# A near mask on GpSimd, a second bank for small tiles' transposes, and outputs weighted on ScalarE in the sparse attention

## What is computed

```python
logits = jnp.einsum('bqgrd,bqkgd->bqgrk', q_b, k_sel).astype(jnp.float32) * scale
bias = t5_table[t5_bucket(sel - tpos[None, :, None])]
logits = logits + bias.astype(jnp.float32)
logits = jnp.where(valid[:, :, None, None, :], logits, -jnp.inf)
p = jax.nn.softmax(logits, axis=-1).astype(v.dtype)
o = jnp.einsum('bqgrk,bqkgd->bqgrd', p, v_sel)
```

## Time and profile before

| | us |
|---|---|
| median of 3 executions (2685.77 to 2688.29) | 2685.83 |
| the profiled execution: its own time | 2684.7 |
| its span from first to last instruction | 2682.9 |
| of it `dsa_phase` | about 321 |
| PE busy in the span | 2594.0 (97%) |
| DVE, ACT, POOL busy | 1578.9, 1265.8, 1454.0 |

### The profile page before, as it was taken

One profiled execution on the slowest core, in us unless ns is written; L12 is line 12 of the kernel. 1 busy time (PEld: TensorE's weight loads), 2 busy tenths in 40 slices (PEclk: granted clock), 3 DMA queues, 4 the chain that ended last, 5 costly groups with the idle time before them and its releaser, 6 DMA issues. The chain is left out here.

```text
span 2682.9 us, 40475 instructions
## 1 busy us (share of the span) xinstructions
PE 2594.0 (97%) x14062; PEld 2256.1 (84%) x14062; DVE 1578.9 (59%) x2722; ACT 1265.8 (47%) x2823; POOL 1454.0 (54%) x1057
## 2 busy tenths in 40 slices
PE   6799899999999999999999999999999999999999
PEld 6699788898878888888789999999878788888877
DVE  5899877763665656556641114666448655556656
ACT  5678566662333333333445556777425333333332
POOL 2044433202557777777844444556217767777773
PEclk9999999999999999999999999999999999999999
DMA  5100000011111121111131110333311111111102
GB/s 182 47 25 24 29 9 5 28 60 48 48 48 48 55 69 48 47 47 47 40 129 48 48 48 21 80 91 80 114 48 48 48 47 47 63 47 51 60 29 94
DMA packets 77358, 147.24 MB, mean 55 GB/s; under 512 B 8528, under 2 KB 45568, under 8 KB 75552
## 3 DMA queue, kind: packets, MB, share of 16 engines
q1 hardware_dynamic: 77216, 145.38, 16.9%
HBM read 122.22 MB, written 13.69 MB: 51 GB/s over the span
## 5 line engine op out<-in xcount | busy, mean ns | idle before, releaser
L1116 DVE TENSOR_TENSOR XT<-XT,banks 128x1024 f32<-128x1024 f32 x176 | 214.6, 1220 | 210.4 <-PE banks L1021 210.3
L849 POOL TENSOR_TENSOR WL<-WF,WH 128x512 fp32r<-128x512 f32 x164 | 247.7, 1522 | 14.1 <-ACT WH L675 14.1
L849 POOL TENSOR_TENSOR WL<-WRB,WH 128x512 fp32r<-128x512 f32 x108 | 172.8, 1616 | 146.2 <-ACT WH L669 140.1
L987 PE MATMUL banks<-XH,WH 128*128 128x512 f32 x608 | 237.7, 391 | 5.0 <-ACT U L699 5.0
L849 POOL TENSOR_TENSOR WL<-WR,WH 128x512 fp32r<-128x512 f32 x98 | 198.8, 2051 | 76.6 <-ACT WH L669 76.6
L987 PE MATMUL banks<-XL,WH 128*128 128x512 f32 x608 | 237.2, 390 | 0.0
L987 PE MATMUL banks<-XH,WL 128*128 128x512 f32 x608 | 237.1, 390 | 0.0
L1021 PE MATMUL banks<-AH,WH 128*128 128x512 f32 x640 | 200.0, 394 | 6.1 <-DVE XT L1116 4.4
L1100 DVE SCALAR_TENSOR_TENSOR YG<-U,CONVW,YG 128x1023 f32<-128x1023 f32 x88 | 179.4, 2039 | 31.4 <-ACT YG L714 31.4
L1021 PE MATMUL banks<-AL,WH 128*128 128x512 f32 x640 | 197.5, 390 | 0.0
L1021 PE MATMUL banks<-AH,WL 128*128 128x512 f32 x640 | 197.1, 389 | 0.0
(11 more groups left out here) (442 smaller groups left out, 7525.1 us busy)
## 6 DMA issues: line engine op xcount, KB each, us to landing
WR<-in_up SPq DMA_DIRECT2D x44, 512.0 KB, 4.7
WRB<-in_up SPq DMA_DIRECT2D x44, 512.0 KB, 4.2
WF<-in_down SPq DMA_DIRECT2D x88, 256.0 KB, 2.6
HT<-HC SPq DMA_DIRECT2D x224, 64.0 KB, 2.0
QWR<-in_qkv SPq DMA_DIRECT2D x8, 1536.0 KB, 6.3
XT<-in_xT SPq DMA_DIRECT2D x16, 512.0 KB, 7.9
QWR1F<-in_qkv SPq DMA_DIRECT2D x4, 1536.0 KB, 6.4
spill<-XT SPq DMA_DIRECT2D x8, 512.0 KB, 11.0
```

Source lines behind the costliest of these rows:

```text
L849: pool.tensor_tensor(out_, src, hi.bitcast(F32), ALU.subtract).then_inc(signal, 1)
L987: mm = pe.matmul(BANK[bank], w[:, n, b * P:(b + 1) * P], x[:, b, :], start=(first and b == 0 and w is WH and x is XH[i]), stop=(b == 3 and ...
L1116: dve.tensor_tensor(c.XT[:, db, :], c.XT[:, db, :], DN[db % 2][:], ALU.add).then_inc(dn_free, 1)
```

## The change

Three moves, all in `dsa_phase`:

1. The mask of the near 256 keys is no longer added on PE. GpSimd adds it to the bias instead (`near_mask`, 96 instructions of 128 x 256, into a ring `NEAR` of 3), and `row_max` takes `NEAR` in place of `BB`. It waits for `near_ready`.
2. For tiles 0 to 2 the odd rounds (output and keys) are transposed into `TP[1]`, which those tiles leave unused, so that they need not wait for the copies of the queries out of `TQ`.
3. `output` on DVE keeps the reciprocal alone. ACT weighs the output (`weigh`), one instruction of 64 columns per head, ahead of `exp(g + 2)` in even steps.

```diff
+        NEAR = m.take("NEAR0", [P, AHEAD, W], F32)
...
-        RCP = m.take("RCP0", [P, 2], F32)
+        RCP = m.take("RCP0", [P, 2, 2], F32)
...
+        LAST_SIDE = 2
+        def on_side(g):
+            return g % 2 == 1 and place(g)[3] <= LAST_SIDE
+        def seat(g):
+            return TP[1] if on_side(g) else TQ
+        def seat_free(g):
+            earlier = [v for v in range(g) if has_round(v) and on_side(v) == on_side(g)]
+            return rounds_before(earlier[-1] + 1) if earlier else 0
...
+            def weigh(o):
+                act.wait_ge(rcp_done, o + 1)
+                act.wait_ge(pv_ready, 2 * o + 2)
+                for h in range(2):
+                    mm = act.activation(MO[:, o % 2, h * HD:(h + 1) * HD], OP[:, h * HD:(h + 1) * HD], ACT.Copy,
+                                        scale=RCP[:, o % 2, h:h + 1])
+                mm.then_inc(mo_ready, 1)
...
+                if h == 0 and g >= 2:
+                    weigh(g // 2 - 1)
                 if g + 2 < ALL:
                     exp(g + 2)
...
+            def near_mask(g):
+                p, k, s, i, h = place(g)
+                if i < FIRST_TOP:
+                    return
+                n, v = masked_before(g), (i + 1) * P - W
+                if p == 0:
+                    pool.wait_ge(mask_ready, i - FIRST_TOP + 1)
+                else:
+                    pool.wait_ge(b_masked, p)
+                if n >= AHEAD:
+                    pool.wait_ge(max_done, unmasked[n - AHEAD] + 1)
+                pool.tensor_tensor(NEAR[:, n % AHEAD, :], BB[p % 2][:, h, S - W:S],
+                                   MASK[:, SC_OFF[i] + v:SC_OFF[i] + v + W], ALU.add).then_inc(near_ready, 1)
...
             for t in range(EARLY, TT):
+                near_until(2 * t - 4)
                 scaled(t)
...
             for k in range(1, GROUPS):
+                base = 2 * UNITS * (k - 1)
                 for i in range(TT + 1):
+                    near_until(13 + 2 * (i // 2) if k == 1 else base + 2 * i + 3)
                     if i < TT:
                         raw_square(k * TT + i)
+                    if k > 1:
+                        near_until(base + 2 * i + 5)
                     if i >= 1:
                         root(k * TT + i - 1)
                     if i in (1, 2):
                         scaled(k * TT + i - 1)
                 for i in range(2, TT):
+                    near_until(base + UNITS + 2 * i + 2)
                     scaled(k * TT + i)
+            near_until(ALL)
...
-                hidden = i >= FIRST_TOP
-                if hidden:
-                    pe.wait_ge(mask_ready, i - FIRST_TOP + 1)
...
-                    mm = pe.matmul(blocks, q, keys[:, :, 1, :], start=False, stop=not covered)
-                    if covered:
-                        mm = pe.matmul(LG[g % 2][:, m0:b], c.IDB[:], MASK[:, SC_OFF[i] + m0:SC_OFF[i] + b],
-                                       start=False, stop=True)
+                    mm = pe.matmul(blocks, q, keys[:, :, 1, :], start=False, stop=True)
...
+                if i == 4 and g % 2 == 0:
+                    pe.wait_ge(turned_lo, rounds_before(g - 2 * (4 - LAST_SIDE) + 2))
...
+                    near_bias = NEAR[:, masked_before(g) % AHEAD, :]
+                    dve.wait_ge(near_ready, masked_before(g + 1))
...
                 dve.wait_ge(exp_done, 2 * o + 2)
-                dve.reciprocal(RCP[:], SUM[:, c0:c0 + 2]).then_inc(rcp_done, 1)
-                dve.wait_ge(rcp_done, o + 1)
-                dve.wait_ge(pv_ready, 2 * o + 2)
-                dve.tensor_tensor(MO[:, o % 2, :].rearrange("p (h d) -> p h d", h=2),
-                                  OP[:, 0:PAIR].rearrange("p (h d) -> p h d", h=2),
-                                  RCP[:].unsqueeze(2).to_broadcast([P, 2, HD]), ALU.mult).then_inc(mo_ready, 1)
+                if o >= 2:
+                    dve.wait_ge(mo_ready, o - 1)
+                dve.reciprocal(RCP[:, o % 2, :], SUM[:, c0:c0 + 2]).then_inc(rcp_done, 1)
```

More of the change, by code:

```diff
@@ L1920, in masked_before @@
             return sum(place(v)[3] >= FIRST_TOP for v in range(g))
+        unmasked = [v for v in range(ALL) if place(v)[3] >= FIRST_TOP]
         def seconds_before(g):
@@ L1964, in queries_high, with others_high @@
                                scale=c.HGAIN[:, 0:1]).then_inc(turned_hi, 1)
[L1966 removed]
+            def others_high(t, o, r, bank):
                 act.wait_ge(turned, r + 1)
                 if o is not None:
[L1969 removed]
+                    mm = act.activation(c.MH[:, o // TT, o % TT * P:(o % TT + 1) * P], bank[:, 0:P], ACT.Copy)
                 if t is not None:
[L1971 removed]
+                    mm = act.activation(KHL[:, t // TT % 2, t % TT, 0, :], bank[:, P:2 * P], ACT.Copy,
                                         scale=c.HGAIN[:, 1:2])
                 mm.then_inc(turned_hi, 1)
+            def weigh(o):
[5 more added lines that the diff above has]
+                mm.then_inc(mo_ready, 1)
             exp(0)
@@ L2029, in scaled, with near_until @@
                     ALU.mult).then_inc(dup_ready, 1)
+            nears = 0
+            def near_until(g_end):
+                nonlocal nears
+                while nears < min(g_end, ALL):
+                    near_mask(nears)
+                    nears += 1
             for t in range(EARLY, TT):
+                near_until(2 * t - 4)
                 scaled(t)
@@ L2050, in _, with queries @@
         def _(pe):
-            def queries(t, r):
+            def queries(t, g):
                 pe.wait_ge(dup_ready, t - EARLY + 1)
-                if r >= 1:
-                    pe.wait_ge(turned_lo, r)
+                if seat_free(g):
+                    pe.wait_ge(turned_lo, seat_free(g))
                 for j in range(NQ):
@@ L2057, in queries, with others @@
                 mm.then_inc(turned, 1)
-            def others(t, o, r):
-                pe.wait_ge(turned_lo, r)
+            def others(t, o, bank, free):
+                if free:
+                    pe.wait_ge(turned_lo, free)
                 if o is not None:
                     pe.wait_ge(mo_ready, o + 1)
-                    mm = pe.transpose(TQ[:, 0:P], MO[:, o % 2, :], c.IDF[:])
+                    mm = pe.transpose(bank[:, 0:P], MO[:, o % 2, :], c.IDF[:])
                 if t is not None:
-                    mm = pe.transpose(TQ[:, P:2 * P], DUP[:, t % 2, NQ * PAIR:NH * PAIR], c.IDF[:])
+                    mm = pe.transpose(bank[:, P:2 * P], DUP[:, t % 2, NQ * PAIR:NH * PAIR], c.IDF[:])
                 mm.then_inc(turned, 1)
@@ L2096, in turn @@
                     pe.wait_ge(pt_dve, seconds_before(g))
+                if i == 4 and g % 2 == 0:
+                    pe.wait_ge(turned_lo, rounds_before(g - 2 * (4 - LAST_SIDE) + 2))
                 for b in range(i + 1):
-                    bank, seat = divmod(b, cut(i + 1))
-                    mm = pe.transpose(TP[bank][:, seat * P:(seat + 1) * P], PR[:, g % AHEAD, b * P:(b + 1) * P],
+                    bank, row = divmod(b, cut(i + 1))
+                    mm = pe.transpose(TP[bank][:, row * P:(row + 1) * P], PR[:, g % AHEAD, b * P:(b + 1) * P],
                                       c.IDF[:])
@@ L2127, in _ @@
                     if g % 2 == 0:
-                        queries(tile_of(g), rounds_before(g))
+                        queries(tile_of(g), g)
                     else:
-                        others(tile_of(g), output_of(g), rounds_before(g))
+                        others(tile_of(g), output_of(g), seat(g), seat_free(g))
             values(ALL - 1)
@@ L2163, in queries_low, with others_low @@
                                          ALU.subtract).then_inc(turned_lo, 1)
-            def others_low(t, o, r):
+            def others_low(t, o, r, bank):
                 dve.wait_ge(turned_hi, r + 1)
@@ L2168, in others_low @@
                     cols = slice(o % TT * P, (o % TT + 1) * P)
-                    mm = dve.tensor_tensor(c.ML[:, o // TT, cols], TQ[:, 0:P], c.MH[:, o // TT, cols].bitcast(F32),
+                    mm = dve.tensor_tensor(c.ML[:, o // TT, cols], bank[:, 0:P], c.MH[:, o // TT, cols].bitcast(F32),
                                            ALU.subtract)
@@ L2172, in others_low @@
                     keys = KHL[:, t // TT % 2, t % TT]
-                    mm = dve.scalar_tensor_tensor(keys[:, 1, :], TQ[:, P:2 * P], c.HGAIN[:, 1:2],
+                    mm = dve.scalar_tensor_tensor(keys[:, 1, :], bank[:, P:2 * P], c.HGAIN[:, 1:2],
                                                   keys[:, 0, :].bitcast(F32), ALU.mult, ALU.subtract)
@@ L2198, in row_max @@
                     dve.wait_ge(far_done, masked_before(g + 1))
-                dve.tensor_tensor_reduce(out=PR[:, g % AHEAD, far:n], in0=LG[g % 2][:, far:n],
-                                         in1=BB[p % 2][:, h, S - n + far:S], op0=ALU.add, op1=ALU.min, scale=-1.0,
+                    near_bias = NEAR[:, masked_before(g) % AHEAD, :]
```

(4 more changed lines are left out.)

20 lines of the change are left out of this document (9 added, 11 removed).

## The result

| | before | changed |
|---|---|---|
| median of 20 executions each, us | 2685.79 | 2689.74 |
| lowest to highest, us | 2683.03 to 2691.92 | 2686.35 to 2694.88 |
| span of the profiled execution, us | 2682.9 | 2687.4 |
| PE busy in it, us | 2594.0 | 2586.4 |

The ratio is 1.0015 with a 95% interval of 1.0009 to 1.0021: slower by 3.95 us. PE has 7.6 us less to do and ends 4 us later.

What follows compares the result with a forecast made beforehand. PE was taken as the bound, with rings through TQ, OP and DVE setting the small tiles' steps. Pair terms +1.0 + 0 + 0.4 - 2.2 - 1.0 = -1.8 us gave 2684.0 us, range 2677 to 2690.

Steps and rivals of the forecast that it cites:

- The mask on PE: Each 256-column mask matmul taken off PE saves 0.12 us; 11.4 us of PE in all, 1.4 in each pair.
- The near mask on POOL: 96 new POOL instructions at 0.70 us each, 67 us in all, with ends at 0.5 and 1.26 us.
- There before DVE asks: POOL's near masks ready in time in pairs 1 to 7; in pair 0 late squares make DVE wait some 1.0 us.
- Pairs 6 and 7: -0.5 us each: PE 0.42 us late after tile 2, then eight masks take off 0.94.
- Pairs 2 and 4: +0.2 us each: +0.52 from the ring with the variance as far as tile 3, -0.36 from masks in tiles 4 to 6.
- the output ring: Cycle through output bank OP (reciprocal, weighting, PE): 0.53 us before, 0.75 with weighting on ACT, longer by 0.22 us.
- Pairs 3 and 5: -1.1 us each: PE 0.4 us ahead at tile 4, then six masks worth 0.72 us.
- at tile 4 PE is 0.4 us ahead, then six masks come off undisturbed: Step for pairs 3 and 5: nothing delays PE from tile 4, so the masks' 0.72 us adds to the 0.4.
- Pairs 0 and 1: Pair 0 +1.0 us, PE's 0.2 to 0.4 lateness from weightings given back by masks; pair 1 at 0, between -1.1 and +0.5.
- The number of turns: Some 23 turns of an output ring bound PE, among them 3 in each of pairs 6 and 7, 4 in 2 and 4.
- Rival (b): Slower: ACT's weighting is dearer, or its wait for values holds the exponential; 2695 us at 1.0 us a pair; chance 0.07.
- rival (d): Second bank for small tiles does nothing; pairs 3 and 5 lose their 0.4 us, 2684.8 us; chance 0.69 together with the forecast.

Runs made afterwards that it cites:

- e6: Whole change with POOL's order in pair 0 mended, plus DVE's reciprocal one step earlier than in that mended kernel; 2677.23 us, ratio 0.9953 to 0.9978.
- e8: Whole change with POOL's order in pair 0 mended, ACT's weighting moved behind the even step's exponential; 2686.24 us, one execution.
- e5: Near mask and second bank on the kernel before, POOL's order in pair 0 mended, weighting left on DVE; 2676.02 us, ratio 0.9953 to 0.9978.
- e3: Weighting on ACT alone, on the kernel before; 2694.30 us, ratio 1.0022 to 1.0050.
- e9: e5 with the variance's scale-and-add on DVE in a three-operand form; 2676.88 us, ratio 0.9952 to 0.9978.
- e10: e6 with the variance in three-operand form and, in pairs 2 and 4, scaled copies behind their near masks; 2673.03 us, ratio 0.9931 to 0.9958.

## Why the prediction was wrong

- **The mask on PE, 0.12 us.** Right: steps that run dense, as tile 5's second, fell by 0.13, and pairs 6 and 7 by 1.2 with this part alone.
- **The near mask on POOL.** Duration right (0.67 for 0.70). "There before DVE asks" was right in pairs 1 to 7 and wrong in pair 0, where only the order of the squares was looked at, and not what stands ahead of the near mask of step 13. What PE lost by waits was still near the 1.0 us forecast (1.07, both waits of DVE together). What came on top was 1.4 us at the lower clock.
- **Pairs 6 and 7.** The sum is right, -0.46 and -0.44 for -0.5, but by two errors that meet: tiles 0 to 2 lost 0.24 us (0.42 forecast, since tile 0's ring too passes over a masked product), and tiles 3 to 6 gained 0.69, not 0.94.
- **Pairs 2 and 4.** Forecast +0.2, measured +0.43. The missed term is the variance held by POOL: 0.33 and 0.28 us in place of 0.17 at the two tiles where it lies in the output ring, together 0.27 us, about the 0.23 that were missed. The prediction asked of POOL's new work only whether it was in time, not whom it disturbs.
- **Pairs 3 and 5.** The step of the prediction that failed is "at tile 4 PE is 0.4 us ahead, then six masks come off undisturbed". Up to tile 1 the trace follows the forecast to 0.03 us. But at tile 4 PE is level with the kernel before (17.26 us behind the pair's start, 17.28 before), not 0.4 us ahead: tile 2's second step waits for the weighted output (0.35 us) and takes 2.56 us in place of 2.06, tile 3's 2.80 in place of 2.38. By the spacing of PE's starts the waits in the second steps are 0.49 us at tile 3 (for the copy of the queries, none before), 0.46 at tile 4 (0.05 before) and 0.42 at tile 6 (0.28 before), and of the 0.72 only 0.06 is left. They come by way of the exponential that the weighting holds: with the reciprocal early (e6) these steps took 2.25, 2.87 and 3.03 us, as long as before or less, and with the exponential ahead of the weighting (e8) 2.30, 2.87 and 3.03.
- **Pairs 0 and 1.** The same term, where ACT has also the masks and the weight blocks to do: 2.6 us each, where 0.2 to 0.4 and "between -1.1 and +0.5" stood. In pair 0 the queue without a gap counts by itself: with the reciprocal early, 1.1 of the 2.6 us stay (41.49 in e6, 40.39 in e5), in pair 1 0.26.

All in all the term that turned the forecast was the weighting on ACT: priced at its 0.41 us of queue and 0.22 us a turn of the output ring (5 us), it cost 11.8. The number of turns was right, and where nothing else waits each is 0.22 us longer, as forecast (e3, pair 6, second steps of tiles 0, 1 and 2); what had no price was the time that ACT stands with all its queue behind it until DVE's reciprocal is there. Rival (b) had named the mechanism ("its wait for values holds the exponential") but priced it only by a longer instruction; and the wait that mattered was for the reciprocal, which stood behind DVE's low copies, themselves behind ACT's. On DVE the weighting followed its reciprocal in one queue and waited for nobody; on ACT the wait between the two kept the exponential. The second bank was undersized too: 4.3 us alone, where the prediction saw 0.2 us at the turn of tile 1 and 0.4 in each of pairs 3 and 5 (0.8 in all by rival (d)), since it took the longer output ring to stop the gain at once. That the total still fell inside the range is in part luck: the two errors have opposite signs.

What stays open: whether most executions of the changed kernel have the stretch at the lower clock, why the rest of the program had more or less of it from trace to trace, and why DVE started late in pair 3 of e9 and pair 5 of e10.

## What to carry to other kernels

An instruction that is moved to another engine takes its waits with it. Price the time it stands there, with all that is queued behind it, and not only the time it takes; then make what it waits for early. Here taking a reciprocal one step sooner was worth 12 us, three times what the whole change lost. And ask of work given to an idle GpSimd not only whether it is ready in time but which of VectorE's instructions run beside it.
